# Hybrid decode step on one Trainium2 core: the first pair's mask, turning and value steps moved one row tile later

## The chip, the cores and the metric

The kernel runs on one core of a Trainium2 chip. The metric is the device time of one launch in microseconds (us), lower is better. Five engines work side by side and meet only at semaphores: TensorE (PE in the profile; PEld is its weight load), VectorE (DVE), ScalarE (ACT), GpSimd (POOL) and SyncE (SP). SP, POOL and ACT also issue the transfers between device memory and on-chip memory, each in its own order.

## What is computed

One inference step of a two-layer decoder trunk, for 512 prompt rows and 64 sample rows (8 sequences of 8 new positions, each with 2048 cached positions in 16 pages).

```
h = RMSNorm(x); z = h @ W_in             # 1024 -> 3912 columns, partitioned
A: an indexer scores all keys, top-k selects them (128 of the prompt, 256 of the sample),
   softmax attention (8 heads x 64) over the selected keys only
B: causal pooling windows 2/4/8/16, minus self, then a small product
C: chunked spatial gating, lower-triangular 128x128 weights per head
y = concat(A, B, C branches, each * silu(gate)); out = y @ W_out; x = x + RMSNorm(out)
```

Everything is in float32. For the sample rows the keys of branch A come from paged caches: every page of K and of V is read whole, the unselected positions are masked.

## The kernel before, in words

**Rows and tiles.** The 576 rows make five row tiles: four of 128 prompt rows and one of 64 sample rows (`ST`, written 4 below). In each layer the work of TensorE is a list of 50 *tiles* (function `_layer`): 40 input products (`z`: a chunk of W_in times a row tile) and 10 output products (`out`: half of W_out times a row tile). A product for 128 rows is eight k-steps and some 7 us long (line 1490; 1847 for the output); one for the sample rows is 64 small ones and 3.6 us long (line 1473). The tiles are numbered 0 to 49 within a layer. In the stretch of the change they are: 15 to 19 `k` (15 is the sample rows'), 20 to 24 `v` (20 is the sample rows'), 25 to 29 `uv` (29 the sample rows'), 30 to 34 `ga` (34), 35 to 39 `xg` (39), 40 to 49 the output products.

**Order by hand.** Between two tiles stand small steps, in five parts: FRONT (0), ROWS_A (1), COLS (2), ROWS_B (3), BACK (4). `put(n, part, step)` places a step behind tile n. Every engine walks the same list `STEPS` and does its share of each step in that order, so a step that is moved is moved in the queue of every engine. That holds for POOL too: weight loads (`load_w`, line 705) are issued when the walk comes to the tile that frees the slot, page loads (line 722) and key loads (line 624) when it comes to their steps. SP has a list of its own: key loads for the layer (line 624), then page loads (line 667).

**The sample attention** goes by four pairs of sequences. For each pair:
- `K p,j` (j = 0..3, line 1507): queries times 8 pages of keys, 2 MB for each step, then `snew`, the new keys (line 1520);
- `mk p,j` (line 1739 on TensorE, 1160 on VectorE): the selection mask is added and a maximum taken; `mx` joins the maxima; `exp` (line 1007, ScalarE) makes the weights;
- `turn p,j` (lines 1565, 1567): the weights are transposed, ScalarE copies them out (line 923);
- `V p,j` (line 1542): transposed weights times 8 pages of values, 2 MB each; `V p,4` the new values (line 1553); then `od` (VectorE, line 1177) and `yo` (line 1749 on TensorE, 1369 on VectorE).

Every K and V step with pages is a *page step*, 32 in a layer; `PLACES` names the tile behind which each stands. Four buffers of two pages each are reloaded (by SP and POOL, half each) as soon as the step before has used them, so two page steps in a row leave one tile's time for 2 MB.

**The prompt's selection.** `pi i,c` (line 1723 on TensorE, 992 on ScalarE, 1382 on VectorE) makes the scores of row tile i, in twelve steps; `psel` (lines 1396 and 1399) finds the top 128 by 16 rounds of eight maxima on VectorE: for row tile 1 at tiles 20 to 22, for row tiles 2 and 3 together at tiles 24 to 28, three rounds each (four at 28). `pmask` (line 1402) turns the result into the mask, and `L i,c` (line 1759 on TensorE, 1211 on VectorE) makes the prompt's logits, from tile 30 on with that mask.

**From layer to layer.** The indexer keys of the next layer are loaded into buffers that this layer's last pair has used. `keys_free` says when: for pairs 2 and 3 after `turn 3,*` and `yo 3` on TensorE, for pairs 0 and 1 after `gT 3`, `yT` and `gaS`. SP then issues 64 key loads of 32 KB. POOL issues its `pool keys` at steps 45 to 49, and between them, behind tile 47, the load of the next layer's first weight chunk (`kg`, tile 0 of the layer). The indexer's scores `S` (line 1591) stand behind tile 6 of the layer and wait for all keys; SP starts the page loads of the layer after them.

`norm` and `res` (lines 909 and 1184 to 1189; 1053 and 1268 to 1276) are the norms before and after a layer; `yT` (1831), `gaS` (1790), `gT` (1784) and `xT` (1666) are transposes.

**Banks.** ScalarE's results stand in two banks in turn (`z`, `T`, `K`, `snew`, `turn`, `P`, `out` use them), VectorE's in three. A tile can start only when the use before last of its bank has been copied out by ScalarE.

Of the kernel before, what the change touches and what calls it, by code (L numbers as in the profile page):

```python
# [33 lines left out]
ST = PT_TILES  # L34
# [26 lines left out]
def _pack():  # L61
# [25 lines left out]
    for w in WINDOWS:  # L87
# [53 lines left out]
        for ends in (((ST, 0), (ST, 1), (3, 1)), ((3, 1), (ST, 0), (ST, 1)))]  # L141
# [2 lines left out]
KEY_STEPS = [("keys", 1, pair, j) for pair in (0, 1) for j in range(NCH)]  # L144
POOL_KEYS = [("pool keys", 1, pair, j) for pair in (2, 3) for j in range(NCH)]

TURNS_AT = ((20, 0, 0, (0,)), (20, 4, 0, (1,)), (21, 4, 0, (2,)), (22, 4, 0, (4, 3)),
# [3 lines left out]
MASKS_AT = ((0, (18, 4), (19, 0), 19), (1, (20, 0), (20, 4), 21), (2, (29, 4), (30, 0), 30), (3, (36, 4), (37, 0), 37))  # L151

PLACES = [10, 11, 12, 13, 14, 16, 17, 18, 20, 21, 22, 23, 24, 25, 26, 27, 28, 30, 31, 32] + list(range(33, 45))
PI_PLACES = [(n, part) for n in (18, 19, 20, 21, 22, 23) for part in (1, 3)]


def _layer(l):
# [16 lines left out]
    FRONT, ROWS_A, COLS, ROWS_B, BACK = range(5)  # L174

    def put(n, part, *steps, layer=l):
        slots[n][part].extend((s[0], layer) + s[1:] for s in steps)
# [51 lines left out]

    places = list(PLACES)  # L230
    for kind, p in PAGE_SEQ:
        for j in range(NCH):
            n = places.pop(0)
# [7 lines left out]
    put(17, COLS, ("snew", 0), ("snew", 1))  # L241
    for n, part, p, js in TURNS_AT:
        if (n, part) != (38, FRONT):
            put(n, part, *[("turn", p, j) for j in js])
    for p, (n, part), (n2, part2), n3 in MASKS_AT:
        put(n, part, *[("mk", p, j) for j in range(3)])
        put(n2, part2, *[("mk", p, j) for j in range(3, NCH + 1)], ("mx", p))
        put(n3, ROWS_B, ("exp", p))
    pairs = [(i, c) for i in range(1, PT_TILES) for c in range(NC4)]
    for (n, part), (i, c) in zip(PI_PLACES, pairs):  # L250
        put(n, part, ("pi", i, c))
# [14 lines left out]
    for n, rt in enumerate(RTP):  # L266
        put(33 + n, COLS if rt == ST else FRONT, ("sg", rt))
        n = at["xg", rt]
# [8 lines left out]
        put(n, FRONT, ("gT", i))  # L277
    put(38, BACK, ("xl", 0), ("xl", 1), ("gpost",))
    put(43, BACK, ("ldsmall",), ("xl", ST), ("xl", 2), ("xl", 3))
    put(45, ROWS_A, ("yT", ST), ("gaS",))  # L280
    for n, part, p, js in TURNS_AT:
        if (n, part) == (38, FRONT):
            put(n, part, *[("turn", p, j) for j in js])
# [21 lines left out]


STEPS = [s for l in range(DEPTH) for s in _layer(l)]


# [1581 lines left out]
```

How the kernel before makes its waits and increments, by code:

```python
        def keys_free(eng, l, pair):  # L628
            if l == 0:
                return
            if pair < 2:
                eng.wait_ge(dve_free, max(dve_emptied("gT", l - 1, 3), dve_emptied("yT", l - 1, ST), dve_emptied("gaS", l - 1)))
            else:
                eng.wait_ge(act_full, max(act_filled("turn", l - 1, 3, j) for j in range(NCH + 1)))
                eng.wait_ge(dve_full, dve_filled("yo", l - 1, 3))
# [2 lines left out]
        @block.sync  # L639
        def _(sp):
            sp.dma_start(table[0:1, :], page_order).then_inc(table_in, 16)
            def load_rows(rt):
                sp.dma_start(X[rt][0:rows(rt), :], x_rows(x_prompt, x_sample, rt)).then_inc(x_in[rt], 16)
            load_rows(ST)
            load_rows(0)
            load_rows(1)
            sp.wait_ge(table_in, 16)
            for rt in (2, 3):
                load_keys(sp, mybir.EngineType.SP, 0, 2, 0, ki_in, (rt - 2,))
                load_rows(rt)
# [10 lines left out]
            def load_groups(cache, l, nos, used):  # L662
                for gi in (0, 2):
                    if used is not None:
                        sp.wait_ge(group_used, used + gi)
                    for e in range(2):
                        sp.dma_start(PG[2 * gi + e], cache[l, bass.ds(nos[2 * gi + e], 1), :, :].rearrange("o p n -> p (o n)"))\
                            .then_inc(group_in[gi], 16)
# [20 lines left out]
        @block.gpsimd  # L689
# [131 lines left out]
            pool.wait_ge(st_cv, 16 * DEPTH)  # L821
            for i in range(5):
                pool.wait_ge(st_x[i], 16)
```

## Time and profile before

| | |
|---|---|
| three runs | 1001.85, 1000.95, 998.19 us; median 1000.95 |
| profiled execution | 999.5 us |
| its span in the profile | 997.8 us |
| granted TensorE clock, mean | 0.994 |
| TensorE busy | 934.6 us of the span |
| VectorE, ScalarE, GpSimd busy | 535.9, 305.4, 272.6 us |
| moved by DMA | 205 MB, 206 GB/s mean |

The span is what the profiler saw between the first and the last instruction; the launch is 1.7 us longer. Times in the rows are us from the start of the span. Layer 0 runs up to about 510, layer 1 from there. A timeline row has: start, duration, engine, line, operation, what it writes and reads, count, and in brackets the idle time ahead of it with what ended it. TensorE's durations overlap by pipelining, so the starts are what to subtract.

### The profile page before, as it was taken

The page shows a single profiled execution, that of the slowest core. Times are in us where ns is not written, and L with a number is a line of the kernel's source. Part 1 is how long each engine was busy: PE and PEld are TensorE (multiplying, and loading weights), DVE is VectorE, ACT ScalarE, POOL GpSimd, SP SyncE. Part 2 cuts the span into 40 slices and gives each one's busy share as a digit, 9 for nine tenths or more (in the row PEclk, how much of TensorE's full clock was granted, in tenths as well). Part 3 has the DMA queues.
Part 4 walks back from the last instruction along what each step waited for, and adds up shares of the span by engine and source line. Part 5 has one row for each costly group of instructions (what it writes and reads, how often), then busy time and mean ns, then how long its engine had stood idle before and what let it go on. Part 6 is the DMA issues. An engine that isn't in the chain of part 4 may idle for free.

```text
span 997.8 us, 20531 instructions
## 1 busy us (share of the span) xinstructions
PE 934.6 (94%) x7100; PEld 483.7 (48%) x7100; DVE 535.9 (54%) x1718; ACT 305.4 (31%) x674; POOL 272.6 (27%) x484
## 2 busy tenths in 40 slices
PE   5798999999999999998999999999999999999996
PEld 3434444444454555554555444444445455555543
DVE  4336999475883233233444499966678623332232
ACT  3121121432124245423231211225212424543312
POOL 8710232232222211413342013223222222241110
PEclk9899999999999999999999999999999999999998
DMA  9841677576866655856584338766677667566551
GB/s 314 166 134 43 211 265 250 187 245 226 295 212 212 240 191 186 305 165 222 149 246 128 110 105 280 249 226 207 244 262 246 198 214 249 167 229 247 170 179 53
DMA packets 91954, 205.21 MB, mean 206 GB/s; under 512 B 15047, under 2 KB 26550, under 8 KB 91858
## 3 DMA queue, kind: packets, MB, share of 16 engines
q0 software_dynamic: 38944, 123.98, 36.5%
q1 hardware_dynamic: 47778, 75.78, 23.2%
q10 hardware_dynamic: 5136, 4.20, 1.5%
q8 instruction: 57, 0.93, 0.4%
q14 instruction: 39, 0.32, 0.1%
HBM read 193.88 MB, written 10.14 MB: 204 GB/s over the span
## 4 chain that ended last, share of the span: by engine, by line
PE 74%; DMA 8%; ACT 5%; DVE 4%; issue 4%; ACTq 3%; SPq 1%; POOL 0%; POOLq 0%; DVEq 0%
PE bank L1490 36%; PE bank L1847 10%; PE bank L1507 5%; PE bank L1542 5%; DMA pg<-in_cache_k_dram 4%; PE bank L1473 4%; ACTq L624 2%; PE bank L1723 2%; DMA pg<-in_cache_v_dram 2%; PE bank L1759 2%; PE bank L1591 2%; DMA r<-in_x_prompt_dram 2%; PE bank L1649 1%; PE bank L1565 1%; DVE r L1399 1%
## 5 line engine op out<-in xcount | busy, mean ns | idle before, releaser
L1490 PE MATMUL bank<-wr,ht 128*128 128x512 f32 (+1 forms) x1024 | 436.2, 579 | 5.3 <-DVE ht L1198 2.0
L1490 PEld LDWEIGHTS bank<-wr,ht 128*128 128x128 f32 x1024 | 190.8, 191 | 219.2 <-issue 202.7
L705 POOL DMA_DIRECT2D wr<-in_w_in_dram x50 | 37.1, 742 | 293.0 <-PE bank L1490 225.2
L722 POOL DMA_DIRECT2D pg<-in_cache_v_dram x128 | 69.8, 546 | 165.1 <-PE bank L1542 121.3
L722 POOL DMA_DIRECT2D pg<-in_cache_k_dram x128 | 69.5, 543 | 83.3 <-PE bank L1507 59.2
L1116 DVE TENSOR_SCALAR_CACHE_REDUCE r<-r,sel_i 128x1088 bf16<-128x1088 f32 x62 | 82.8, 1336 | 0.0
L1507 PE MATMUL bank<-pg,qbx 128*32 128x256 f32 x1024 | 63.4, 383 | 7.6 <-DMA pg<-in_cache_k_dram 4.2
L1473 PE MATMUL bank<-wr,ht 128*32 128x256 f32 (+1 forms) x1152 | 65.2, 379 | 2.9 <-DMA wr<-in_w_in_dram 2.6
L1542 PE MATMUL bank<-pg,rs 128*32 128x256 f32 x1024 | 62.3, 382 | 1.8 <-DMA pg<-in_cache_v_dram 1.8
L1847 PE MATMUL bank<-wr,qt 128*128 128x512 f32 x128 | 58.4, 599 | 1.8 <-ACT rs L923 1.8
L1847 PE MATMUL bank<-wr,ht 128*128 128x512 f32 x128 | 57.5, 592 | 0.0
L1399 DVE MATCH_REPLACE8 r<-m,r 128x384 f32<-128x384 f32 (+1 forms) x96 | 51.6, 542 | 0.0
L1396 DVE MAX8 m<-r 128x8 f32<-128x384 f32 (+1 forms) x96 | 50.5, 554 | 1.7
L1473 PEld LDWEIGHTS bank<-wr,ht 128*32 128x32 f32 x1152 | 38.1, 113 | 26.2 <-DMA wr<-in_w_in_dram 3.9
L1211 DVE CUSTOM_DVE_ANT_0 r<-bank,r 128x256 f32<-128x256 f32 (+2 forms) x48 | 24.8, 554 | 42.3 <-PE bank L1759 42.3
L1542 PEld LDWEIGHTS bank<-pg,rs 128*32 128x32 f32 x1024 | 30.0, 109 | 35.5 <-issue 7.1
L1507 PEld LDWEIGHTS bank<-pg,qbx 128*32 128x32 f32 x1024 | 30.1, 109 | 35.4 <-DMA pg<-in_cache_k_dram 5.9
L1382 DVE SCALAR_TENSOR_TENSOR r<-za,wi,r 128x256 f32<-128x256 f32 (+2 forms) x42 | 25.9, 618 | 31.1 <-ACT za L992 30.2
L880 ACT ACTIVATE za<-bank 128x512 f32<-128x512 f32 x16 | 9.6, 597 | 104.4 <-PE bank L1490 104.4
L624 POOL DMA_DIRECT2D sh<-in_cache_kidx_dram x64 | 34.9, 547 | 22.3 <-PE bank L1831 12.7
L880 ACT ACTIVATE zb<-bank 128x512 f32<-128x512 f32 x16 | 9.6, 597 | 100.5 <-PE bank L1490 100.5
L1000 ACT ACTIVATE sh<-bank 128x512 f32<-128x512 f32 x32 | 19.1, 597 | 65.8 <-PE bank L1507 65.8
(271 smaller groups left out, 1167.3 us busy)
## 6 DMA issues: line engine op xcount, KB each, us to landing
pg<-in_cache_k_dram SPq DMA_DIRECT2D x128, 256.0 KB, 5.0
pg<-in_cache_k_dram POOLq DMA_DIRECT2D x128, 256.0 KB, 5.8
pg<-in_cache_v_dram SPq DMA_DIRECT2D x128, 256.0 KB, 5.0
pg<-in_cache_v_dram POOLq DMA_DIRECT2D x128, 256.0 KB, 5.8
wr<-in_w_in_dram POOLq DMA_DIRECT2D x40, 512.0 KB, 4.2
wr<-in_w_in_dram POOLq DMA_DIRECT2D x6, 1024.0 KB, 6.0
wr<-in_w_in_dram POOLq DMA_DIRECT2D x2, 2048.0 KB, 16.6
wr<-in_w_out_dram POOLq DMA_DIRECT2D x8, 512.0 KB, 4.1
```

What stands on the lines that cost most here:

```text
L624: eng.dma_start(KX[pair][par * HD:(par + 1) * HD, c0:c0 + PAGE], kidx_t[l, bass.ds(nos[u * 4 + par * 2 + e], 1), :, :].rearrange("o d n -> ...
L705: pool.dma_start(W[n % 2][:, k, d0:d0 + w], src[k.start * P:k.stop * P, c0:c0 + w].rearrange("(k p) n -> p k n", p=P))\
L722: pool.dma_start(PG[2 * gi + e], cache[l, bass.ds(nos[2 * gi + e], 1), :, :].rearrange("o p n -> p (o n)"))\
L1116: then(nc.vector.tensor_scalar(MSK, SC, scalar, None, ALU.is_ge, ALU.add, accum_out=CNT))
L1382: ins = nc.vector.scalar_tensor_tensor(SCP[i], z, wcol, SCP[i], ALU.mult, ALU.add)
L1396: ins = nc.vector.max(M8[:, (i - 1) * 8:i * 8], SCP[i])
L1399: ins = nc.vector.match_replace(SCP[i], M8[:, (i - 1) * 8:i * 8], SCP[i], -3e38)
L1473: mm = pe.matmul(b[r0:r0 + 32, 0:w // 2], lhs(k)[:, r:r + 32], weights[:, k, t * (w // 2):(t + 1) * (w // 2)], start=(k == 0), stop=(k == ...
L1490: mm = pe.matmul(b[0:m, 0:w], HT[:, k, rt * P:rt * P + m], W[n % 2][:, k, 0:w], start=(k == 0), stop=(k == KC - 1))
L1507: mm = pe.matmul(bk[r0:r0 + 32, u * 256:(u + 1) * 256], QBX[:, 2 * e + k, 2 * p + par, :], two[par][:, :, 2 * e + k, :], start=(k == 0), s ...
L1542: mm = pe.matmul(acc[r0:r0 + 32, :], RS[n % 2][:, c0:c0 + 32], PG[2 * gi + e][:, g * DP:(g + 1) * DP], start=(j == 0 and u == 0 and e == 0 ...
L1847: mm = pe.matmul(b[:, :], lhs, W[n % 2][:, k, :], start=(k == 0), stop=(k == KC - 1))
```

## The change

The page steps that stood at tile 20 and later are redistributed: none at 20 any more, one more at 45, so `V 0,0` stands at 21 instead of 20, `V 0,3` at 24 instead of 23, `K 2,0` at 25 instead of 24, `V 1,0` at 30 instead of 28, and the rest one tile later up to `V 3,3` at 45 instead of 44. `od` and `yo` follow the last V step of their pair: `yo 3` stands at 46 FRONT instead of 45 FRONT. The masks of pairs 0, 1 and 3 are one tile (or half a one) later, those of pair 2 stay; the turnings are moved with them. The prompt's score steps `pi` at 20 move to 21 and the later ones to 22, 23 and 24, so `pi 3,2` and `pi 3,3` stand at 24 instead of 23; `psel` stays where it was, and so do all weight loads and key steps. `gaS` moves from 45 to 46. No operation is added or removed.

```diff
-TURNS_AT = ((20, 0, 0, (0,)), (20, 4, 0, (1,)), (21, 4, 0, (2,)), (22, 4, 0, (4, 3)),
-            (27, 4, 1, (0,)), (29, 4, 1, (1,)), (30, 4, 1, (2,)), (31, 4, 1, (4, 3)),
-            (36, 4, 2, (0,)), (37, 4, 2, (1,)), (38, 0, 2, (2,)), (39, 4, 2, (4, 3)),
-            (40, 4, 3, (0,)), (41, 4, 3, (1,)), (42, 4, 3, (2,)), (43, 4, 3, (4, 3)))
-MASKS_AT = ((0, (18, 4), (19, 0), 19), (1, (20, 0), (20, 4), 21), (2, (29, 4), (30, 0), 30), (3, (36, 4), (37, 0), 37))
-
-PLACES = [10, 11, 12, 13, 14, 16, 17, 18, 20, 21, 22, 23, 24, 25, 26, 27, 28, 30, 31, 32] + list(range(33, 45))
-PI_PLACES = [(n, part) for n in (18, 19, 20, 21, 22, 23) for part in (1, 3)]
+TURNS_AT = ((21, 0, 0, (0,)), (21, 4, 0, (1,)), (22, 4, 0, (2,)), (23, 4, 0, (4, 3)),
+            (29, 4, 1, (0,)), (30, 4, 1, (1,)), (31, 4, 1, (2,)), (32, 4, 1, (4, 3)),
+            (37, 4, 2, (0,)), (38, 0, 2, (1,)), (39, 4, 2, (2,)), (40, 4, 2, (4, 3)),
+            (41, 4, 3, (0,)), (42, 4, 3, (1,)), (43, 4, 3, (2,)), (44, 4, 3, (4, 3)))
+MASKS_AT = ((0, (19, 4), (20, 0), 20), (1, (21, 0), (21, 4), 22), (2, (29, 4), (30, 0), 30), (3, (37, 4), (38, 0), 38))
+
+PLACES = [10, 11, 12, 13, 14, 16, 17, 18] + list(range(21, 29)) + list(range(30, 46))
+PI_PLACES = [(n, part) for n in (18, 19, 21, 22, 23, 24) for part in (1, 3)]
...
-    put(45, ROWS_A, ("yT", ST), ("gaS",))
+    put(45, ROWS_A, ("yT", ST))
+    put(46, ROWS_A, ("gaS",))
```

## Rows read from the trace of the kernel before

**Rows 1.** The page, its first part: busy time and share of the span.

```profile
PE 934.6 (94%) x7100; PEld 483.7 (48%) x7100; DVE 535.9 (54%) x1718; ACT 305.4 (31%) x674; POOL 272.6 (27%) x484
```

**Rows 2.** Timeline of TensorE from tile 43 of layer 0 to layer 1's scores.

```profile
468.44 3.70 PE L1847 MATMUL bank<-wr,qt 128*128 128x512 f32 x8 [1.83 <-ACT rs L923]
...
486.09 0.53 PE L1749 MATMUL bank<-cst,sh 128*128 128x32 f32 x4
...
495.39 1.93 PE L1473 MATMUL bank<-wr,small 128*32 128x256 f32 x32
...
510.84 8.99 PE L1490 MATMUL bank<-wr,ht 128*128 128x328 f32 x32
...
545.10 1.95 PE L1591 MATMUL bank<-gr,small 64*64 64x512 f32 x16
```

**Rows 3.** Timeline of SP's queue in the same stretch: the next layer's key loads.

```profile
487.43 27.87 SPq L624 DMA_DIRECT2D sh<-in_cache_kidx_dram x32
516.07 26.10 SPq L624 DMA_DIRECT2D gr<-in_cache_kidx_dram x32
```

**Rows 4.** Windows of 0.2 us ahead of the scores; the last two columns are DMA share, GB/s.

```profile
543.60:543.80 0.20, 0.20 (x2) 0.08 (x1) 0.00 (x0) 0.00 (x0) 0.00 (x0) 1.00 0.05 13
543.80:544.00 0.20, 0.20 (x2) 0.11 (x1) 0.00 (x0) 0.00 (x0) 0.00 (x0) 1.00 0.00 0
```

**Rows 5.** Timeline of GpSimd in the same stretch: key loads and a weight load.

```profile
487.94 2.31 POOL L624 DMA_DIRECT2D sh<-in_cache_kidx_dram x4 [12.71 <-PE bank L1831]
...
499.81 1.82 POOL L705 DMA_DIRECT2D wr<-in_w_in_dram x2
```

**Rows 6.** The page, DMA issues: the weight pieces of 1 MB, time to landing.

```profile
wr<-in_w_in_dram POOLq DMA_DIRECT2D x6, 1024.0 KB, 6.0
```

**Rows 7.** Timeline of VectorE, tiles 23 to 30 of layer 0.

```profile
238.88 1.54 DVE L1382 SCALAR_TENSOR_TENSOR r<-za,wi,r 128x512 f32<-128x512 f32 x2 [0.84 <-ACT za L992]
...
245.12 0.22 DVE L1369 COPY small<-bank 128x64 f32<-128x64 f32 x1 [4.05 <-PE bank L1749]
...
254.57 0.29 DVE L1211 CUSTOM_DVE_ANT_0 r<-bank,cst 128x128 f32<-128x128 f32 x1 [1.84 <-PE bank L1759]
...
286.37 0.29 DVE L1211 CUSTOM_DVE_ANT_0 r<-bank,cst 128x128 f32<-128x128 f32 x1 [2.05 <-PE bank L1759]
```

**Rows 8.** Timeline of TensorE, tiles 23 to 34 of layer 0.

```profile
234.23 1.93 PE L1542 MATMUL bank<-pg,rs 128*32 128x256 f32 x32
...
236.53 1.13 PE L1723 MATMUL bank<-r 64*128 64x512 f32 x4
...
244.56 0.53 PE L1749 MATMUL bank<-cst,sh 128*128 128x32 f32 x4
...
256.51 1.07 PE L1507 MATMUL bank<-pg,qbx 128*32 128x256 f32 x16 [1.08 <-DMA pg<-in_cache_k_dram]
...
302.09 0.70 PE L1759 MATMUL bank<-kt,qt 64*128 64x256 f32 x2 [1.16 <-DVE sst L1160]
...
346.46 1.07 PE L1507 MATMUL bank<-pg,qbx 128*32 128x256 f32 x16 [0.76 <-DMA pg<-in_cache_k_dram]
```

**Rows 9.** Timeline of TensorE, layer 1: tiles 30, 34 and 44.

```profile
784.10 0.70 PE L1759 MATMUL bank<-kt,qt 64*128 64x256 f32 x2 [1.16 <-DVE sst L1160]
...
827.95 1.07 PE L1507 MATMUL bank<-pg,qbx 128*32 128x256 f32 x16 [1.24 <-DMA pg<-in_cache_k_dram]
829.59 1.07 PE L1507 MATMUL bank<-pg,qbx 128*32 128x256 f32 x16 [0.57 <-DMA pg<-in_cache_k_dram]
...
958.89 1.07 PE L1542 MATMUL bank<-pg,rs 128*32 128x256 f32 x16 [1.31 <-DMA pg<-in_cache_v_dram]
```

**Rows 10.** Layer 0's first tiles: TensorE's longest wait, then windows (columns: PE busy, clock, DMA share, GB/s).

```profile
46.13 1.11 PE L1697 MATMUL bank<-cst,vt 64*128 64x64 f32 x8 [6.45 <-DVE small L1303]
...
44.00:46.00 2.00, 0.00 (x0) 0.50 0.81 202
...
48.00:50.00 2.00, 2.00 (x5) 0.50 0.77 214
```

## The prediction

> **What bounds the kernel now.** I read the page first, then the chain of waits, then TensorE's waits one by one in its timeline, then the queues of the others around each. TensorE is busy 934.6 of 997.8 us [rows 1], and the change neither adds nor removes an operation. So its time can only go where TensorE waits: 63 us in all, of which about 18 lie in the first 46 us and 8 behind the last product, out of the change's reach. What it can touch is some 35 us in pieces of 0.2 to 1.9 us. The forecast is a balance of such pieces, and of one new wait at the layer boundary. The half per cent that a measurement of this kernel can tell from no change is 5 us.
>
> **The layer boundary (once: layer 0 to 1).** What is late here is `yo 3`. Before, it follows tile 45, at 486.09 [rows 2]. SP's first key load of the next layer starts at 487.43, and its 64 loads run without a gap to 542.2, 0.82 to 0.87 us each [rows 3]: SP is bound by issuing, not by the transfers. The last traffic ends at about 543.7 [rows 4], and `S`, which waits for all keys, starts at 545.10 [rows 2]. So the slack is 1.4 us, and every delay of `yo 3` beyond that is a wait of TensorE at `S`.
>
> How late is `yo 3` after? It then stands at the end of tile 46, which before is where tile 47 starts, 495.39 [rows 2]. The work ahead of that point is the same as before, save that `yo 3` and `gaS` go behind it (0.4 us each, by the distance of such groups in row 486.09's neighbourhood). One wait goes too: tile 44 waits 1.83 us [rows 2], because its bank is the one that `turn 3,4` used, and ScalarE copies that only behind `norm 0` and `res 1`. After, a single `turn 3,2` stands there, tile 44's bank is then that of tile 43's product, long copied, and the wait is gone. The same pair of turnings stands one tile later behind `norm 1` alone; I give it 0.15 us. `V 3,2` at tile 44 loses the cover of that wait for its pages: 0.2 us, between 0 and 1. Sum: 495.39 - 0.8 - 1.83 + 0.35 = 493.1, against 486.25: **6.8 us later**. Less the slack of 1.4: `S` starts 5.4 us later than before, everything in between included. Bounds: 4.4 (more of SP's start hidden) and 7 (no slack, a slower landing).
>
> Two things lie inside this and don't add. `gaS` ends right ahead of tile 47, which needs VectorE's result: 0.7 us, where it was covered by tile 46 before. And POOL is moved as well: its `pool keys` wait for `yo 3`, at 487.94 before, 494.7 after. It is in-order, and 11.9 us of key issues stand ahead of the load for tile 0 of layer 1 [rows 5], so this goes from 499.81 to 506.7. Two pieces are issued, 1.8 us, and the 1 MB one lands 6.0 us after its issue [rows 6]: 513.6. TensorE is at tile 0 at 510.84 before [rows 2] and about 510.1 after: a wait of some 3.5 us. It comes to `S` at about 547.9, where the keys hold it until 550.5, 2.6 us more. The later of the two, SP's keys, sets the end.
>
> **TensorE's clock.** In layer 0's start TensorE idled for 6.45 us, and the granted clock was 0.50 (1.2 GHz) at the end of that and still in 48 to 50, after it had been at work again from 46.13 [rows 10]. A wait of 3.5 us may or may not do that; if so, some 4 us at half speed cost 2 us, and `S` would have to wait 0.6 instead of 2.6. Where I costed this at nothing, the cover is the wait for keys. The Trainium skill (TensorE: Matmul & The Clock Gate, section "HAM oscillation") holds that waits between bursts of matmuls send the array back to half rate until it has been busy again; the trace agrees for 6.45 us, and no row shows it for 3.5. By that rule the sum stays and its margin shrinks.
>
> **Tiles 20 to 30 (each layer).** In the first part (20 to 23) the same steps meet the same banks one tile later, and I count nothing: the waits at `pi` and at the turnings behind tile 22 recur. Then two things meet.
> - A gain. `K 2,1` waited 1.08 us for its pages at tile 25, one tile after `K 2,0` [rows 8]. After, `K 2,0` is at 25, behind `V 0,3`, `V 0,4`, `pi 3,3`, a full tile and `yo 0`: 2 us more for the same 2 MB, so no wait.
> - A cost. VectorE's `psel` of row tiles 2 and 3 starts before at about 245.3, as soon as `yo 0` arrives (245.12 [rows 7]). After, it waits for `pi 3,3` at 24 ROWS_B, behind two V steps. Tile 24 ends 4.0 us earlier than 244.56, since a V step of 1.9 and two `pi` steps of 1.1 now come later [rows 8]: at 240.6. Then `pi 3,2` 1.1, V 1.9 and 0.4, `pi 3,3` 1.1, ScalarE's copies 1.1, VectorE's two multiply-adds 1.5 and the mask 0.3 [rows 7, 8]: 248. **VectorE starts 2.7 us late.**
> From there to the mask of pair 2 at 302, VectorE has 56.7 us, of which it waits 6.8 for TensorE, in four gaps of which the first is 1.84 and the last 2.05 [rows 7]. After, this idle time is what takes up the 2.7 us: 248 + 50 + 0.3 = 298.4 for `L 1,0`. Before it stands at 302.09, with a wait of 1.16 for VectorE [rows 8]. By then TensorE has a V step and a turning less behind it (2.4 us, to be done later). So the net gain is 3.7 - 2.4 = **1.3 us in layer 0**. VectorE bounds this stage. In layer 1 the page wait of 1.08 is not there, the wait of 1.16 is [rows 9]; the same sum gives **0.6**. Bounds: from no gain to 2.7 in layer 0 (all of 1.08, 0.45 at a turning, 1.16), to 1.6 in layer 1.
>
> **Tile 34 (each layer).** The sample rows' tile is short, and the page step behind it waits 0.76 in layer 0 [rows 8] and 1.24 + 0.57 = 1.8 in layer 1 [rows 9]. After, it is `K 3,0`, and between it and the page step before stand also `V 1,4` and `yo 1`, 0.8 us: **0.76 and 0.8** gained. Bounds: nothing, and all 2.6.
>
> **Tiles 35 to 42.** Here TensorE waits behind each product until ScalarE has loaded a table and copied the gates, about 2.26 us behind its end. The masks of pair 3 leave that shadow at tile 37 and enter it at 38, `yo 2` leaves it at 41 and enters at 42: nothing, plus or minus 0.4.
>
> **Tile 44, 45, layer 1.** `V 3,3` waited 1.31 us at 44 [rows 9]. `V 3,2` takes its place with one short turning less of cover: **0.3 lost**. `V 3,3` at 45 and the end of the kernel: nothing, since `gaS` is used only at tile 48 there.
>
> **Sum.** 5.4 - 1.3 - 0.76 - 0.6 - 0.8 + 0.3 = +2.2 us on the profiled execution (999.5 to 1001.7; span 997.8 to 1000.0). That execution was 1.45 us under the median of the three runs, 1000.95, so the forecast against the median is **1003.2 us**.
>
> **Rivals.**
> 1. *The boundary is free.* If the keys are taken up elsewhere (a longer slack, faster issues) and the weights land in time, `S` is 0.8 us earlier and all else as above: -4.0, so 997 us. For it: SP's start is only inferred from the order of events, and the queue could run on. Against it: SP's issues are gapless, and the rows leave 1.4 us. The chance is 0.14. It also holds the case that the change does less than it says.
> 2. *The page waits move on instead of going.* The 2 MB per tile are then late at 34 whatever stands ahead: +1.6 over the forecast, 1004.8. For it: waits of this kind recur at short tiles. Chance 0.12.
> 3. *Slower: VectorE's selection becomes the bound for good.* Place: tiles 24 to 30 in each layer. The four gaps of 6.8 us are waits for `L`, and `L` is tied to TensorE's own place; if half of them stays although `psel` starts 2.7 us late, each layer's `L 1,0` comes 3.4 us later: +6.8 over the forecast, 1010 us. It decides from the point where the late start exceeds what the gaps give back, 2.7 us. For it: in tile 28 the sum leaves VectorE only 0.3 us idle. Against it: TensorE arrives earlier as well. Chance 0.14.
> 4. The forecast: 0.60.
>
> **Range and chances.** The forecast's own bounds run from -2 to +6 us, 999 to 1007. To 997 it takes in half of rival 1, to 1010 rival 2 and half of rival 3. Left out are 0.07 and 0.07 of these, and 0.04 of tails: 997 to 1010. Faster by over 5 us (under 996): 0.06 of rival 1, 0.01 of the forecast, 0.07. Slower by over 5 us (over 1006): 0.13 of rival 3, 0.03 of rival 2, 0.02 of the forecast, 0.18. Within: 0.75.
>
> **What would show it.** Right: in the changed kernel's timelines, no wait for ScalarE at tile 44 of layer 0; SP's key loads start about 6.8 us after their old place relative to tile 44; TensorE waits for weights ahead of layer 1's first product (about 3.5) and for keys ahead of `S` (about 2.6); VectorE starts `psel` of two row tiles behind the scores, with gaps of under 1 us up to tile 30; no page wait at tile 25. Wrong: `S` at its old place (the boundary is then free), a wait for VectorE of over 2 us at tile 30 (rival 3), or page waits of their old size at 34 (rival 2).

## Result and profile after

The changed kernel took 1008.0 us (median of 8 runs, 1005.15 to 1011.33) against 1001.99 for the kernel before in the same comparison (8 runs): a ratio of 1.0058, 95% interval 1.0041 to 1.0076. In a second comparison, made later with the same two kernels (experiment 12 has the control for it), it took 1005.77 against 1002.46: 1.0030, interval 1.0014 to 1.0046. So the change costs some 3 to 6 us. The forecast was 2.2 us: the sign, the main place and the range were right, the size was too small.

The profiled execution of the changed kernel took 1011.33 us, the slowest of its eight; its span is 1009.6. The times of single stretches below are therefore read together with a second profiled execution (experiment 11). All lines of the code stand one later than before. The busy row of its page, against [rows 1]: TensorE's 7 us more are not more work but the same products at a lower clock (mean granted clock 0.988, before 0.994).

```profile
PE 941.5 (93%) x7090; PEld 485.0 (48%) x7100; DVE 536.4 (53%) x1718; ACT 306.1 (30%) x674; POOL 272.6 (27%) x484
```

**Where the time is.** Three starts of TensorE cut an execution into stretches that can be compared: tile 15 of layer 0 (ahead of all that the change moves), tile 43 of layer 0, and the start of the scores `S` of layer 1. Each number is the difference of two starts in TensorE's timeline, the last the span less the start of `S`. Both kernels were profiled twice.

| | tile 15 starts | tile 15 to 43 | tile 43 to `S` | `S` to end |
|---|---|---|---|---|
| before | 145.80 | 311.2 | 88.1 | 452.7 |
| before, second execution | 145.31 | 311.4 | 91.1 | 452.5 |
| changed | 150.18 | 306.4 | 98.3 | 454.8 |
| changed, second execution | 147.51 | 307.0 | 98.5 | 452.7 |

The first column is chance: nothing ahead of tile 15 was changed. In these rows, the first of the kernel before and the other two of the changed one, the wait for VectorE is 7.38 us instead of 6.45 [rows 10], and the product behind the wait for weights takes 5.21 instead of 3.66:

```profile
85.53 3.66 PE L1473 MATMUL bank<-wr,ht 128*32 128x256 f32 x64 [2.61 <-DMA wr<-in_w_in_dram]
...
47.73 1.11 PE L1698 MATMUL bank<-cst,vt 64*128 64x64 f32 x8 [7.38 <-DVE small L1304]
...
88.15 5.21 PE L1474 MATMUL bank<-wr,ht 128*32 128x256 f32 x64 [2.56 <-DMA wr<-in_w_in_dram]
```

In the table, work of 2.4 us has left the second column for the third: a page step of 1.9 us and a turning of 0.5 now stand behind the start of tile 43. Less that, layer 0's middle gained 2.4 us (and 2.0 in the second pair), and the stretch to `S` lost 7.8 and 5.0.

**The boundary, against [rows 2].** TensorE's timeline of the changed kernel:

```profile
465.91 3.60 PE L1848 MATMUL bank<-wr,qt 128*128 128x512 f32 x8
...
485.84 1.07 PE L1543 MATMUL bank<-pg,rs 128*32 128x256 f32 x16 [0.70 <-DMA pg<-in_cache_v_dram]
488.00 1.07 PE L1543 MATMUL bank<-pg,rs 128*32 128x256 f32 x16 [1.10 <-DMA pg<-in_cache_v_dram]
...
496.41 0.53 PE L1750 MATMUL bank<-cst,sh 128*128 128x32 f32 x4
...
497.93 1.93 PE L1474 MATMUL bank<-wr,small 128*32 128x256 f32 x32 [0.60 <-ACT bank L944]
...
517.64 10.78 PE L1491 MATMUL bank<-wr,ht 128*128 128x328 f32 x32 [4.37 <-DMA wr<-in_w_in_dram]
...
554.85 3.04 PE L1592 MATMUL bank<-gr,small 64*64 64x512 f32 x16 [2.05 <-DMA gr<-in_cache_kidx_dram]
```

Read it from the top: tile 44 has lost its wait of 1.83. `V 3,3`, now at tile 45, waits twice for its pages, 1.80 together. `yo 3` stands at 496.41. Tile 47 waits 0.60 behind `gaS`. Layer 1's first products wait 4.37 for weights, and two of them together take 10.78 where they took 8.99. The scores wait 2.05 for keys. SP's queue, against [rows 3]:

```profile
497.76 27.52 SPq L625 DMA_DIRECT2D sh<-in_cache_kidx_dram  x32
526.93 26.26 SPq L625 DMA_DIRECT2D gr<-in_cache_kidx_dram  x32
```

It starts 41.2 us behind tile 43, where it was 30.4, and ends at 553.19, 1.7 us ahead of the scores. `gaS` ahead of tile 47 was forecast at 0.7. GpSimd, against [rows 5], waits 19.61 us for TensorE ahead of its first key load and issues the weights at 509.73:

```profile
498.25 2.68 POOL L625 DMA_DIRECT2D sh<-in_cache_kidx_dram  x4 [19.61 <-PE bank L1791]
...
509.73 1.83 POOL L706 DMA_DIRECT2D wr<-in_w_in_dram  x2
```

And the clock around the two waits, in windows of 2 us (columns: length, PE busy, granted clock, DMA share, GB/s). It stands at 0.50, 1.2 GHz, behind each of them:

```profile
514.00:516.00 2.00, 0.00 (x0) 1.00 1.04 354
516.00:518.00 2.00, 0.36 (x1) 1.00 1.07 331
518.00:520.00 2.00, 2.00 (x5) 0.50 1.00 213
520.00:522.00 2.00, 2.00 (x6) 0.64 1.02 330
...
556.00:558.00 2.00, 2.00 (x16) 0.50 0.93 375
558.00:560.00 2.00, 2.00 (x16) 0.76 0.01 4
```

**Layer 0's middle, against [rows 7, 8].** VectorE ends its last multiply-add of the scores at 252.2 and starts the selection at 252.53. From there to 302 its timeline shows no bracket at all: the four gaps of before are gone.

```profile
250.63 1.54 DVE L1383 SCALAR_TENSOR_TENSOR r<-za,wi,r 128x512 f32<-128x512 f32 x2 [0.90 <-ACT za L993]
...
252.53 1.15 DVE L1397 MAX8 m<-r 128x8 f32<-128x384 f32 x2
...
287.15 0.29 DVE L1212 CUSTOM_DVE_ANT_0 r<-bank,cst 128x128 f32<-128x128 f32 x1
```

TensorE's waits there and in layer 1, against [rows 8, 9]:

```profile
302.87 0.70 PE L1760 MATMUL bank<-kt,qt 64*128 64x256 f32 x2 [0.48 <-DVE sst L1161]
347.06 1.07 PE L1508 MATMUL bank<-pg,qbx 128*32 128x256 f32 x16 [0.19 <-DMA pg<-in_cache_k_dram]
...
791.73 0.70 PE L1760 MATMUL bank<-kt,qt 64*128 64x256 f32 x2 [0.25 <-DVE sst L1161]
835.14 1.07 PE L1508 MATMUL bank<-pg,qbx 128*32 128x256 f32 x16 [0.40 <-DMA pg<-in_cache_k_dram]
836.92 1.07 PE L1508 MATMUL bank<-pg,qbx 128*32 128x256 f32 x16 [0.72 <-DMA pg<-in_cache_k_dram]
...
904.56 1.07 PE L1543 MATMUL bank<-pg,rs 128*32 128x256 f32 x16 [1.67 <-DMA pg<-in_cache_v_dram]
...
975.96 1.07 PE L1543 MATMUL bank<-pg,rs 128*32 128x256 f32 x16 [0.38 <-DMA pg<-in_cache_v_dram]
977.84 1.07 PE L1543 MATMUL bank<-pg,rs 128*32 128x256 f32 x16 [0.81 <-DMA pg<-in_cache_v_dram]
```

The wait for pages at tile 25 is gone. Those at tile 34 are smaller. One of 1.67 us is new at tile 39 of layer 1, and the last two rows are `V 3,3` at tile 45 of layer 1.

### The profile page after: what moved, and what is told of

The parts are those of the page before. It is cut to its first block, busy times and chain, and to the rows that moved or that the text cites. A ratio compares the mean times of both kernels' runs of the same rounds, so it can differ in the third digit from the quotient of the medians.

```text
span 1009.6 us, 20520 instructions
## 1 busy us (share of the span) xinstructions
PE 941.5 (93%) x7090; PEld 485.0 (48%) x7100; DVE 536.4 (53%) x1718; ACT 306.1 (30%) x674; POOL 272.6 (27%) x484
## 4 chain that ended last, share of the span: by engine, by line
PE 69%; DMA 8%; DVE 7%; SPq 6%; ACT 4%; issue 4%; ACTq 1%; POOLq 0%; POOL 0%; DVEq 0%
PE bank L1491 34%; PE bank L1848 8%; PE bank L1543 5%; PE bank L1508 5%; SPq L625 4%; DMA pg<-in_cache_v_dram 3%; PE bank L1474 3%; DVE r L1400 3%; DVE m L1397 2%; DMA pg<-in_cache_k_dram 2%; PE bank L1760 2%; PE bank L1724 2%; PE bank L1592 2%; DMA r<-in_x_prompt_dram 2%; PE bank L1566 1%
## 5 line engine op out<-in xcount | busy, mean ns | idle before, releaser
L1491 PEld LDWEIGHTS bank<-wr,ht 128*128 128x128 f32 x1024 | 192.0, 192 | 225.6 <-issue 204.9
L1848 PEld LDWEIGHTS bank<-wr,ht 128*128 128x128 f32 x128 | 24.3, 190 | 30.6 <-issue 30.6
```

The source lines that it names most:

```text
L1491: mm = pe.matmul(b[0:m, 0:w], HT[:, k, rt * P:rt * P + m], W[n % 2][:, k, 0:w], start=(k == 0), stop=(k == KC - 1))
L1848: mm = pe.matmul(b[:, :], lhs, W[n % 2][:, k, :], start=(k == 0), stop=(k == KC - 1))
```

## Experiments

**1. The late `yo 3`, and with it `gaS`, on the kernel before.** All else stays where it was.

```diff
-                    put(n + 1, FRONT, ("yo", p))
+                    put(n + 1 + (p == PAIRS - 1), FRONT, ("yo", p))
...
-    put(45, ROWS_A, ("yT", ST), ("gaS",))
+    put(45, ROWS_A, ("yT", ST))
+    put(46, ROWS_A, ("gaS",))
```

> The kernel before, with one part of the change alone: yo 3 and gaS behind tile 46 instead of 45, all page steps, masks and turnings where they were. Theory (the boundary costs: next layer's key loads, and with them GpSimd's weight load, wait for yo 3): yo 3 moves from 486.25 to about 494.6, 8.3 us; less the slack of 1.4 the scores of layer 1 start 6.9 us later than before; TensorE waits some 4 us for weights ahead of layer 1's first product and 2 to 3 us for keys ahead of the scores, and the clock may fall once or twice, 1 us each. Time: 7 to 9 us over the kernel before, some 1009 to 1011. Rival (the boundary is free, the change's cost lies in pages or in VectorE's selection): within 1 us of the kernel before, about 1002.

Measured: 1008.29 against 1002.79 us, ratio 1.0048 (1.0026 to 1.0069). So these two steps, with all pages, masks and turnings at their old places, cost as much as the whole change. Its timeline of TensorE shows the wait for weights at tile 0:

```profile
518.75 11.04 PE L1491 MATMUL bank<-wr,ht 128*128 128x328 f32 x32 [6.06 <-DMA wr<-in_w_in_dram]
```

The scores had no wait for keys: they start at 554.10, 95.7 us behind tile 43 (88.1 and 91.1 in the two executions of before), and SP had issued its last key load by 551.21. The weights were 6.06 us late, the clock was 0.50 from 516 to 522, and the two products behind the wait took 11.04 us instead of 8.99. The time rose by some 5 us, less than the 7 to 9 expected. In this execution it was the wait for weights that set the boundary, not the one for keys.

**2. The changed kernel with `yo 3` one tile earlier**, at the end of tile 45's steps instead of behind tile 46; `gaS` stays at 46.

```diff
-                    put(n + 1, FRONT, ("yo", p))
+                    put(n + (p < PAIRS - 1), FRONT if p < PAIRS - 1 else BACK, ("yo", p))
```

> The changed kernel with yo 3 taken out of tile 46 FRONT and put at 45 BACK, right behind V 3,4, so that TensorE waits there about 1 us for VectorE's od 3 in each layer, but the key loads start some 7 us earlier. Theory (boundary): the waits of 4.37 us for weights and 2.05 us for keys go, with the 2.9 us that the half clock cost behind them; 2 us are paid for od. Time about 7 us under the changed kernel, 1001, which is 1 us under or at the kernel before. Rival (pages or VectorE's selection are the cause): 1 to 2 us over the changed kernel, about 1010.

Measured: 1001.53 against 1002.79, ratio 1.0000 (0.9982 to 1.0018). The waits for weights and for keys are gone. The price is a wait of `yo` for VectorE's `od` just ahead of it, in each layer:

```profile
485.42 0.60 PE L1750 MATMUL bank<-cst,sh 128*128 128x32 f32 x4 [0.77 <-DVE sh L1178]
```

The page waits at tile 45 are still there (0.62 and 1.18). Experiments 1 and 2 together settle the cause. In the first, `yo 3` and `gaS` are late and the loss is there; in the second, `gaS` is as late as before and `yo 3` is not, and the loss is gone.

**3. The keys without `yo 3`.** For this run three of four key loads of pairs 2 and 3 wait for the last turning alone, and only the last quarter for `yo 3`, whose product reads the buffer that this quarter overwrites.

```diff
             for j in parts:
+                if l > 0 and pair >= 2 and j == NCH - 1:
+                    eng.wait_ge(dve_full, dve_filled("yo", l - 1, 3))
...
                 eng.wait_ge(act_full, max(act_filled("turn", l - 1, 3, j) for j in range(NCH + 1)))
-                eng.wait_ge(dve_full, dve_filled("yo", l - 1, 3))
```

> The changed kernel with the order of all steps kept, but the next layer's keys of pairs 2 and 3 wait only for the last turning; only the last quarter of each, where VectorE's own-heads result lies, still waits for yo 3. Theory (boundary): SP starts about 15 us earlier, after tile 44, stops at yo 3 once, and all keys are there before the scores; GpSimd has three of four key steps out ahead of yo 3, so that the weights for layer 1's first product are at most 1 us late. Both waits and the clock's falls go: 8 to 9 us under the changed kernel, 999 to 1000. The key loads now run beside the page loads of tile 45, whose wait (0.7 + 1.1 us) may grow by up to 2. Rival (pages or selection are the cause): no change, 1008.

Measured: 1003.58, ratio 1.0009 (0.9990 to 1.0029). SP now starts at 477.51, 22.0 us behind tile 43, stops on its way for `yo 3`, and ends at 544.32, 6.3 us ahead of the scores. GpSimd issues the weights at 503.55, 48.0 us behind tile 43 (53.1 in the changed kernel):

```profile
477.51 38.24 SPq L627 DMA_DIRECT2D sh<-in_cache_kidx_dram  x32
...
503.55 1.83 POOL L707 DMA_DIRECT2D wr<-in_w_in_dram  x2 [1.42 <-PE bank L1475]
```

Both waits are gone with `yo 3` left where the change put it. So it is what queues behind `yo 3` that costs, not `yo 3` itself. The early keys are not free either: the page waits at tile 45 grew from 1.8 to 2.84 us (1.01 and 1.83), where key and page traffic now meet. The time is 4 us over the 999 to 1000 expected. The trace also has a wait of 2.08 us named "issue" at a later product (see "Still open").

**4. Small loads out of the pages' way.** The page loads of `V 3,2` and `V 3,3` stand in GpSimd's queue around the input rows and small tables of the next layer. For this run they went from tile 43 to 46, but for one of the three loads of input rows (`xl 2`).

```diff
-    put(43, BACK, ("ldsmall",), ("xl", ST), ("xl", 2), ("xl", 3))
+    put(43, BACK, ("xl", 2))
+    put(46, BACK, ("ldsmall",), ("xl", ST), ("xl", 3))
```

> The changed kernel with GpSimd's small loads for the next layer and two of the three x loads moved from behind tile 43 to behind tile 46. Theory for the page wait at tile 45 of layer 0 (0.70 + 1.10 us in the changed kernel): it comes from these transfers in flight beside the 2 MB of pages; it goes, yo 3 is 1.8 us earlier and so is all that follows, and in layer 1 the wait of 0.38 + 0.81 us at the same tile goes too: 2 to 3 us under the changed kernel, 1005 to 1006. Rival (the page wait comes from the interval alone, one tile of 7 us between two page steps): no change, 1008. The waits for weights and keys stay in either case.

Measured: 1012.28, ratio 1.0095 (1.0063 to 1.0127), the opposite of what was meant. The page waits at tile 45 of layer 0 are gone, so there these loads caused them. In layer 1, where two of three loads of input rows were moved the same way, the wait at this tile was expected to go too, and did not: it is 2.48 us (0.38 + 0.81 in the changed kernel), and 1.26 in experiment 10. Its cause is open. And in layer 0 the small loads now stand in GpSimd's queue ahead of the weights:

```profile
498.11 0.57 POOL L728 DMA_DIRECT2D wt<-in_sgu_w_dram  x1
...
503.13 0.56 POOL L803 DMA_DIRECT2D r<-in_x_prompt_dram  x1
...
509.05 1.83 POOL L707 DMA_DIRECT2D wr<-in_w_in_dram  x2
```

```profile
519.80 11.83 PE L1492 MATMUL bank<-wr,ht 128*128 128x328 f32 x32 [11.93 <-DMA wr<-in_w_in_dram]
```

Ten loads take 5.6 us of GpSimd's issuing (498.11 to 503.69), the weights come 55.8 us behind tile 43 instead of 53.1, and TensorE waits 11.93 us. Tile 0 starts 10.8 us behind their issue, where it was 7.9 and 9.6. `yo 3` was earlier here than in the changed kernel (491.01 against 496.41), and the scores still start 102.7 us behind tile 43 instead of 98.3: the wait for weights alone can set the boundary.

**5. The first part alone.** Masks, turnings, page steps and `pi` of the first pairs one tile later, with an extra page step at tile 29, and from tile 29 on everything as before.

```diff
-TURNS_AT = ((20, 0, 0, (0,)), (20, 4, 0, (1,)), (21, 4, 0, (2,)), (22, 4, 0, (4, 3)),
-            (27, 4, 1, (0,)), (29, 4, 1, (1,)), (30, 4, 1, (2,)), (31, 4, 1, (4, 3)),
+TURNS_AT = ((21, 0, 0, (0,)), (21, 4, 0, (1,)), (22, 4, 0, (2,)), (23, 4, 0, (4, 3)),
+            (28, 4, 1, (0,)), (29, 4, 1, (1,)), (30, 4, 1, (2,)), (31, 4, 1, (4, 3)),
...
+PLACES = [10, 11, 12, 13, 14, 16, 17, 18] + list(range(21, 45))
```

> The change up to tile 28 alone (first pair's masks, turnings and values and the prompt's scores one tile later, the second half of the change taken back): one more page step stands at tile 29, the sample rows' short tile of uv, so that from tile 30 on everything is where the kernel before has it, yo 3 at 45 too. Theory (the boundary carries the loss): no waits for weights and keys there, so no loss of 5 to 6 us. What is left is the middle: 0.6 us gained per layer, against a page wait at tile 29, where 3.6 us of product and 2 us of small steps stand between two page steps that need 8.6: about 3 us in each layer, of which some 1 hides in VectorE's lateness at tile 30. Time: 1 to 5 us over the kernel before, 1003 to 1008, with the boundary's waits absent in the trace. Rival (the first part itself costs, through VectorE's selection): TensorE waits over 2 us for VectorE at tile 30.

Measured: 1007.34 against 1001.65, ratio 1.0065 (1.0040 to 1.0090). The boundary is as before (no wait for weights or keys, 89.2 us from tile 43 to the scores). The largest wait that is new is at tile 29, a product of only 3.6 us with a page step on either side:

```profile
293.52 1.07 PE L1542 MATMUL bank<-pg,rs 128*32 128x256 f32 x16 [2.15 <-DMA pg<-in_cache_v_dram]
```

In layer 1 the same place waits 1.65 and 0.95. These are 4.75 us of a loss of some 6. So the part of the change that skips tile 29 and makes up for it at tile 45 is not decoration: without it, the shift loses in both layers.

**6. The change with the `pi` steps at their old places**, a test of the claim that VectorE's late start bounds tiles 24 to 30.

```diff
-PI_PLACES = [(n, part) for n in (18, 19, 21, 22, 23, 24) for part in (1, 3)]
+PI_PLACES = [(n, part) for n in (18, 19, 20, 21, 22, 23) for part in (1, 3)]
```

> The changed kernel with the prompt's score steps pi back at the tiles of the kernel before (20 to 23), all else as changed. Theory (the last pi, now at tile 24, makes VectorE start psel of row tiles 2 and 3 2.7 us late, and VectorE bounds tiles 24 to 30): VectorE starts psel 2 to 3 us earlier, the waits for VectorE ahead of L 1,0 at tile 30 (0.48 and 0.25 us in the changed kernel) go, and VectorE's gaps at tiles 25 to 28 grow by as much. Tiles 20 to 30 take 0.3 to 0.5 us less in each layer (97.9 and 98.3 in the changed kernel); the time moves by under 1 us. Rival (VectorE is not the bound): the length of tiles 20 to 30 is the same within 0.1 us.

Measured, one execution: 1006.0 us. VectorE starts the selection earlier (101.5 us behind tile 15 instead of 102.4) and has gaps again (0.42, 0.97, 0.94), the wait at `L 1,0` falls to 0.26. But tiles 20 to 30 took 99.05 instead of 97.90 us, because a `pi` product now waits for its bank:

```profile
200.29 0.92 PE L1724 MATMUL bank<-r 64*128 64x384 f32 x4 [1.33 <-ACT za L993]
```

The expected gain did not come. VectorE did bound the stretch in the changed kernel, but in this one execution nothing was gained by freeing it: the `pi` products' own waits took up more than was freed.

**7. Early `yo 3` and late small loads together**, with the small tables behind the weight load this time.

```diff
-                    put(n + 1, FRONT, ("yo", p))
+                    put(n + (p < PAIRS - 1), FRONT if p < PAIRS - 1 else BACK, ("yo", p))
...
-    put(43, BACK, ("ldsmall",), ("xl", ST), ("xl", 2), ("xl", 3))
+    put(43, BACK, ("xl", 2))
+    put(45, BACK, ("xl", ST), ("xl", 3))
+    put(48, BACK, ("ldsmall",))
```

> The changed kernel with yo 3 at 45 BACK, two of the three x loads moved from behind tile 43 to behind tile 45 (ahead of the key steps) and the small loads for the next layer behind tile 48, where they stand behind the first weight load in GpSimd's queue. Theory: as with yo 3 at 45 BACK alone (1001.5), and the page wait at tile 45 of layer 0 (0.62 + 1.18 us) is gone; unlike the version with the small loads behind tile 46, no wait for weights appears, since they no longer stand ahead of the weight load: 999 to 1000, 2 to 3 us under the kernel before. Rival (the small loads behind tile 48 delay the second weight chunk, used at layer 1's tile 3): a wait for weights of over 2 us there and no gain.

Measured: 999.81, ratio 0.9994 (0.9978 to 1.0010). The page waits at tile 45 of layer 0 are gone, the weights are in time; 1.3 us of page waits came up at tile 40 and 0.77 stayed at `od`. No gain can be told from this comparison.

**8. The last pair of turnings at tile 44, on the kernel before**: the wait of 1.83 us [rows 2] by itself.

```diff
-            (40, 4, 3, (0,)), (41, 4, 3, (1,)), (42, 4, 3, (2,)), (43, 4, 3, (4, 3)))
+            (40, 4, 3, (0,)), (41, 4, 3, (1,)), (42, 4, 3, (2,)), (44, 0, 3, (4, 3)))
```

> The kernel before with one step moved: the last two turnings of pair 3 from behind tile 43 to tile 44 FRONT, ahead of V 3,3. Theory (the wait of 1.83 us at tile 44 of layer 0 comes from the bank of turn 3,4, which ScalarE copies only behind norm 0 and res 1): the wait goes, yo 3 and all behind it are 1.8 us earlier, and nothing else moves: 1.5 to 2 us under the kernel before, or less where V 3,3 then waits for its pages, since 1.8 us of their cover is gone: a page wait of 0 to 1 us at tile 44. Rival: the wait only moves to tile 45, no change.

Measured: 1001.95, ratio 1.0003 (0.9985 to 1.0022). The gain of 1.5 to 2 us that was expected did not come: the wait moved by a step instead of going. It is now the turning's own, for its bank, in both layers:

```profile
474.62 0.66 PE L1565 MATMUL bank<-cst,sh 128*128 128x128 f32 x4 [1.24 <-ACT bank L943]
```

**9. The best of both**: as experiment 7, but `yo 3` early in layer 0 alone, since no keys follow layer 1.

```diff
-                    put(n + 1, FRONT, ("yo", p))
+                    put(n + (p < PAIRS - 1 or l == 1), FRONT if p < PAIRS - 1 or l == 1 else BACK, ("yo", p))
```

> The changed kernel with yo 3 at tile 45 BACK in layer 0 alone (in layer 1 at 46 FRONT as in the changed one), the input loads xl 4 and xl 3 at 45 BACK and the small tables at 48 BACK. It differs from the kernel of the earlier run with the early yo and late small loads in layer 1 alone, where that one waited 0.76 us for od at tile 45. Theory 1 (the boundary is the whole loss, and the gains in the tiles 20 to 34 stand): 0.7 us less than that kernel, 998 to 1000, ratio to before 0.996 to 0.999. Theory 2 (what the middle gains is returned as page waits in layer 1 whatever else is done): ratio 1.000 or more.

Measured: 999.43 against 1002.46, ratio 0.9978 (0.9961 to 0.9995), by which it is 2.2 us faster than before. It is the only version here whose interval lies below 1, by little and in one comparison, so a gain is likely and not certain. Its boundary has two short waits and none for weights or keys:

```profile
484.76 0.60 PE L1752 MATMUL bank<-cst,sh 128*128 128x32 f32 x4 [0.77 <-DVE sh L1180]
...
493.31 1.93 PE L1476 MATMUL bank<-wr,small 128*32 128x256 f32 x32 [0.60 <-DVE small L1444]
```

The scores start 91.0 us behind tile 43, of which 2.4 are moved work, and 450.9 us follow, 1.7 less than before; this profiled execution was the fastest of its twelve.

**10. Small loads late, `yo 3` late**: the changed kernel with the loads where experiment 7 has them and `yo 3` at 46 FRONT, so that in layer 0 only the page waits at tile 45 go.

> The changed kernel, with the sample rows' and the last tile's input loads (xl 4, xl 3) at tile 45 BACK and the small tables (ldsmall) at 48 BACK instead of 43 BACK; yo 3 stays at 46 FRONT. It takes the page waits of 0.7 and 1.1 us ahead of tile 46 away without touching the rest. Theory 1 (the two page waits at tile 45 went straight into the boundary, as a term that the prediction had at 0.2): yo 3, SP's key loads and the weight load come about 1.8 us earlier relative to tile 43, the weights wait ahead of layer 1's first product falls from 4.4 to about 3 or less, and the time is 1.5 to 2.5 us under the changed kernel's, near 1006, ratio to before about 1.004. Theory 2 (what the boundary loses is set by the queues alone, so the page waits are only exchanged for a longer weights wait): no change, 1008, ratio 1.006. Theory 3 (the loads at 48 delay other loads): over 1009.

Measured: 1004.3, ratio 1.0023 (1.0002 to 1.0045), against 1005.77 for the changed kernel in the same comparison. SP starts 39.1 us behind tile 43 instead of 41.2 and 41.4, and the scores start 94.8 behind it instead of 98.3 and 98.5.

```profile
491.05 27.76 SPq L627 DMA_DIRECT2D sh<-in_cache_kidx_dram  x32
```

The first theory expected 1.5 to 2.5 us less than the changed kernel. The medians give 1.5, which their intervals do not tell from nothing, and the one trace, of the fastest of twelve executions, gives 3.5 in this stretch. The wait for weights did not fall to 3 us, as the theory had it: it is 4.66, because TensorE comes to it earlier by as much as the weights do.

**11. The changed kernel again.**

> The changed kernel itself once more, for a second profiled execution of it. Theory 1 (the waits are the kernel's, the startup is chance): the page waits at V 3,3 (1.8 together), the wait for gaS at tile 47 (0.6), a weights wait of 3.5 to 5 and a later wait or none at the scores recur, while tile 15 of layer 0 starts anywhere from 145 to 150; from tile 43 of layer 0 to tile 10 of layer 1 it takes 131 to 134.5 us. Theory 2 (part of the boundary's 134.2 us is an accident of that one execution): 130 or less. The median is 1007 to 1009 in both, ratio 1.005 to 1.007.

Measured: 1005.77, ratio 1.0030 (1.0014 to 1.0046). The waits recur, with other sizes. Page waits at tile 45 1.98 together, 6.04 for weights, none for keys:

```profile
484.12 1.07 PE L1543 MATMUL bank<-pg,rs 128*32 128x256 f32 x16 [1.04 <-DMA pg<-in_cache_v_dram]
486.13 1.07 PE L1543 MATMUL bank<-pg,rs 128*32 128x256 f32 x16 [0.94 <-DMA pg<-in_cache_v_dram]
...
517.44 11.30 PE L1491 MATMUL bank<-wr,ht 128*128 128x328 f32 x32 [6.04 <-DMA wr<-in_w_in_dram]
```

The two paths to the scores are that close: the keys, whose last load SP issued at 551.3, and the weights with the slow products behind them, which brought TensorE there at 553.06. In the first execution the keys end last, in the second the weights.

**12. The kernel before again**, against itself.

> The kernel before itself, against itself. It gives a second profiled execution of it and the size of what a comparison shows where nothing differs. Theory 1 (the changed kernel's two ratios, 1.0058 and 1.0030, differ by the spread of single comparisons; the kernel before has the same waits each time): ratio 0.998 to 1.002; tile 15 of layer 0 starts anywhere from 144.5 to 150; from there to the start of the scores of layer 1 it takes 399 to 400 us, with no wait for weights or keys, and from tile 15 to the end of the span 851 to 854. Theory 2 (the first profiled execution of the kernel before was a lucky one, and the difference of 6 to 7 us from tile 15 on that its trace shows against the changed kernel's two is too large): 855 or more from tile 15 to the end of the span.

Measured: 1002.49 against 1002.33, ratio 1.0002 (0.9986 to 1.0018). From tile 15 to the end it took 855.1 us (1000.4 less 145.31), where the first execution took 852.0. So of the two the first was shorter by 3 us, by luck, and all in one stretch: 91.1 instead of 88.1 from tile 43 to the scores. In the second, tile 44 has the same wait as in [rows 2] and takes 5.40 us instead of 3.70, and a wait of 1.65 at the sample rows' `qi` was 0.24 in the first:

```profile
468.17 5.40 PE L1847 MATMUL bank<-wr,qt 128*128 128x512 f32 x8 [1.83 <-ACT rs L923]
...
531.38 3.66 PE L1473 MATMUL bank<-wr,ht 128*32 128x256 f32 x64 [1.65 <-issue]
```

```profile
466.00:468.00 2.00, 0.34 (x4) 1.00 0.96 298
468.00:470.00 2.00, 1.83 (x3) 0.72 0.72 245
470.00:472.00 2.00, 2.00 (x4) 0.50 1.01 388
```

## Why the prediction was right, and where it fell short

**The boundary sets the sign: right.** "What is late here is `yo 3`" held. Experiment 1 gets the whole loss from `yo 3` and `gaS` alone, experiment 2 takes the whole loss away by moving `yo 3` back.

**The sum, stretch by stretch.** The forecast by stretches, 2.4 us of moved work included, and what the mean of the changed kernel's two executions took against before:

| us | forecast | against the first execution of before | against the mean of its two |
|---|---|---|---|
| tile 15 to 43 | -4.5 | -4.5 | -4.6 |
| tile 43 to `S` | +7.8 | +10.3 | +8.8 |
| `S` to end | -1.1 | +1.0 | +1.1 |
| sum | +2.2 | +6.9 | +5.3 |

The middle of layer 0 came out as forecast. Two steps failed: the boundary was costed too low, and layer 1 did not give its gain.

**The boundary's size, 5.4 us: too small, by 1.0 us against the mean of before and 2.5 against its first execution.** From tile 43 to the scores the prediction amounts to 88.1 + 5.4 + 2.4 = 95.9 us, and the two executions took 98.3 and 98.5. Term by term:
- "`V 3,2` at tile 44 loses the cover of that wait for its pages: 0.2 us, between 0 and 1." The page waits came at `V 3,3`, tile 45, which was given nothing: 1.80 and 1.98 us. They stand ahead of `yo 3` and pass into the boundary whole. SP starts 41.2 and 41.4 us behind tile 43, where 30.4 + 6.8 + 2.4 = 39.6 was forecast (the sum took `yo 3` from 486.25; the row has 486.09, which adds 0.2). Experiment 10 took them out, and SP started at 39.1.
- From SP's start to the scores 57.1 us, forecast 56.3 (545.10 + 5.4 less 487.43 + 6.8). The 64 issues took 0.7 us more than in [rows 3].
- The wait for weights, forecast 3.5: 4.4 and 6.0. The issue came 53.1 and 53.3 us behind tile 43 (forecast 42.8 + 6.9 + 2.4 = 52.1), and tile 0 started 7.9 and 9.6 us behind it, not 6.9. The term that was mis-sized is the landing of the weights, 6.0 us, which is the median of six such loads on the page [rows 6]. This load has two pieces, and the second landed 8.4 us behind its issue in the kernel before already (7.8 in its second execution), 6.9 and 8.6 in the changed one. In the trace of before, and then of the changed kernel:

```profile
L705 POOL DMA_DIRECT2D wr<-in_w_in_dram x2: 894/914/934, 499.8 to 500.7; - x2
DMA to landing us min/median/max: 4.4/6.4/8.4
...
L706 POOL DMA_DIRECT2D wr<-in_w_in_dram x2: 897/917/937, 509.7 to 510.7; - x2
DMA to landing us min/median/max: 4.1/5.5/6.9
```

  With the 8.4 us of before, and the second piece's issue moved by 6.9 from 500.7, the sum gives 507.6 + 8.4 = 516.0 and a wait of 5.9 us. That path then comes to the scores at 550.3, as late as the keys (550.5), and with 2 us for the clock it is the later one. What makes this landing longer than the median no run isolates. The DMA share is near 1 in both kernels while the second piece is under way, with key loads beside it (0.97 to 1.12 from 502 to 508 before, 0.97 to 1.07 from 512 to 518 in the changed kernel).
- The slow clock, forecast at 2 us and hidden: two products took 10.78 and 11.30 instead of 8.99, so 1.8 and 2.3 us, and hidden in the first execution. In the second, and in experiment 1, weights and clock together used up the cover of 2.6. The scores themselves ran slow behind their wait in the first (3.04 instead of 1.95). The prediction had weighed the Trainium skill's "TensorE: Matmul & The Clock Gate", section "HAM oscillation", and left open whether it holds for waits this short. The windows of both executions agree with it: the granted clock was 0.50 behind the waits of 4.37 and 6.04 us.

**Tile 44's wait of 1.83 us goes: right** here, since 465.91 has no bracket. Experiment 8 shows that it is no property of the turnings' place alone: with the rest as before it comes back as 1.24.

**Tiles 20 to 30, layer 0: right to 0.1 us.** VectorE was forecast to start 2.7 us late and started 2.9 late (99.5 us behind tile 15 before, 102.4 after). From there to `L 1,0` 50.3 us were forecast and 50.34 taken (302.87 less 252.53). `L 1,0` came 3.6 us earlier behind tile 15 (156.3, then 152.7), less 2.4 of moved work 1.2 (forecast 1.3). In layer 1 it is 0.0 and 0.1 us instead of 0.6: from tile 20 to `L 1,0` before took 109.1 there (110.1 in layer 0), so there was less to gain.

**Tile 34: right in the mean.** The page waits are 0.19 and 1.12 after, 0.39 and 0.59 in the second execution; before, 0.76 and 1.81, and 1.74 and 1.24 in its second. The means are 0.57 and 1.39, so 0.8 a layer.

**Tiles 35 to 42: right in the mean in layer 0.** From the start of tile 35 to that of tile 43 it took 109.1 and 108.4 us before and 108.1 and 108.5 after, 0.5 of which is the turning moved on. In layer 1 a page wait of 1.67 at tile 39 came in one execution, and one of 0.26 in the other. The prediction had nothing for it.

**Layer 1 as a whole: too hopeful, and the second step that failed.** From the scores to the end -1.1 was forecast; against before's 452.6 it was +2.1 and +0.1. Of the 0.6 forecast for tiles 20 to 30 at most 0.1 came. From `L 1,0` to the end (213.7 and 213.2 us before, 217.9 and 216.3 after, of which 2.4 are moved work) it took 2.0 and 0.5 us more, where 0.5 less was forecast. The page wait of 1.67 at tile 39 explains the first; the second is spread over small waits and stays open. The slow scores cost next to nothing: from the scores to tile 20 it took 130.2 and 129.8 us, before 129.9 and 130.2.

**Rivals.** The first (the boundary is free) fell in the changed kernel; experiments 2 and 9 made it true by other means. The second (page waits move on) fell at tile 34 and held at tile 45, a place it did not name. The third (VectorE costs 6.8 more) fell: with the late start every gap closed, as the forecast had it.

**The base.** The sum went against an execution that had no clock fall behind tile 44. Against the mean of the two executions of before (853.6 us from tile 15 to the end) the changed kernel's two (859.4 and 858.3) are 5.3 us longer, against the first alone 6.9. The medians differ by 3 to 6.

**Still open.** The waits at the sample rows' `qi` product (0.24 and 1.65 us before, 2.08 in experiment 3, 1.80 in 9) are named "issue" only, and no run here isolates them. They stand in all eight profiled executions whose weights were in time (0.24 to 2.08 us) and in none of the six that waited for weights (the changed kernel's two, experiments 1, 4, 6 and 10). So a late weight load seems to take the place of this wait, which is 1.2 us in the mean of the eight.

## What to carry to other kernels

When a step moves, look for the queue that waits for it: here a step of 0.5 us on TensorE, one tile later, held back 64 key issues on one queue and a weight load behind others on a second, and the loss was theirs. Follow every path to the next common point and not the longest alone: of two that end within 2 us of each other either can be the later one, and a wait ahead of the step passes into both. Take a load's landing from that load and not from the median of its kind. Profile the kernel before twice before you subtract: of two executions of the same code, one was 3 us longer in the very stretch in question.

## What was not expected of the hardware

TensorE's clock falls behind shorter waits than the start's 6.45 us, and not each time. In the kernel before, the same wait of 1.83 us was followed by a granted clock of 0.50 (470 to 472, experiment 12) in one execution and by full clock in the other. At layer 0's start a wait of 2.61 us was followed by a product of 3.66 us in the kernel before (the row at 85.53 above) and of 5.25 in experiment 5:

```profile
84.36 5.25 PE L1473 MATMUL bank<-wr,ht 128*32 128x256 f32 x64 [2.61 <-DMA wr<-in_w_in_dram]
```

The waits of 4.37, 6.04, 6.06 and 11.93 us ahead of layer 1's first product all had it, and so had 2.05 ahead of the scores. In experiment 9 a wait of 3.05 us at layer 0's start had no fall behind it (the product took 3.66). Behind waits of 1.83 to 2.73 us one fall costs 1.4 to 1.7 us (5.06 less 3.66 in experiment 11, 5.40 less 3.70 in experiment 12), behind those of 4.37, 6.04 and 6.06 it costs 1.8, 2.3 and 2.1 (10.78, 11.30 and 11.04 less 8.99), and behind 11.93 it costs 2.8 (11.83 less 8.99). So a wait of 2 us can cost nearly twice its length, or just its length, in the same kernel. Part of the spread between executions (996.7 to 1002.5 us for the version of experiment 9) may come from this; no run here isolates it.
